# Last pair of experts and three other places reordered in a fused two-block transformer kernel

## The chip, the cores and the metric

The kernel runs on one core of a Trainium2 chip. The core has a matrix engine (PE, whose weight loads are shown as PEld), a vector engine (DVE), a scalar engine (ACT), GpSimd (POOL) and a sync engine (SP) that issues most transfers. The metric is device time in microseconds of one execution of the whole program. All arithmetic is on fp32 data.

## The reference

256 tokens of 1024 features pass through two transformer blocks. The parts that the change touches:

```python
def first_block(x, mem, ...):
    x = x + hybrid_mixer(rmsnorm(x, norm_mix_g), ...)          # mLSTM and spatial gating
    x = x + memory_cross_attention(rmsnorm(x, norm_x_g), rmsnorm(mem, norm_mem_g), w_xq, w_xkv, w_xo)
    x = x + hierarchical_moe(rmsnorm(x, norm_moe_g), w_rg, b_rg, w_re, b_re, w1, w3, w2)
    return rmsnorm(x, norm_f_g)

def memory_cross_attention(xn, mn, w_xq, w_xkv, w_xo):
    q = xn @ w_xq
    k, v = jnp.split(mn @ w_xkv, 2, axis=-1)                   # 4 column blocks of 512: xkv0 to xkv3
    ...

def hierarchical_moe(xn, ...):     # 32 experts of width 512, top 2 of 8 in the best of 4 groups
    ...
    hb = jax.nn.silu(xb @ w1[e]) * (xb @ w3[e])
    return hb @ w2[e]              # gated, and added back to its token's row of x

def second_block(x, c, ctx, ...):
    ada = jax.nn.silu(c) @ w_ada + b_ada       # 12 column blocks of 512: ada0 to ada11
    hc = modulate(rmsnorm(ctx), csh1, csc1); kv_c = hc @ w_in[:, OFF_K:OFF_G]
    ...                                        # Hyena convolution, differential attention, SwiGLU
```

## The kernel before

**Units and the ring.** The weights come in units of 2 MB (8 blocks of 128 rows, 512 columns). `weight_units` lists them in the order in which SP loads them into a ring of five places; unit i of the part before the experts stands in place i mod 5, and its load waits until the unit five before it has been read. SP issues in program order.

**Split products.** Most products are done in three terms, with the weights and the activations each split into a high and a low part in a faster fp32 format. A unit is handled in four quarters: ACT writes the high part (`split_high`, line 2211), DVE the difference (`split_low`, line 1378), PE multiplies (`split_quarter`, line 544). The activations are split likewise, ACT first (2216), then DVE (1384). The high parts of four quarters fit at a time, so ACT makes a quarter's high part when PE has read the quarter four before it.

**Banks.** There are eight PSUM banks. Outside the experts PE takes them in turn, one for each job, in the order in which the jobs are written. It waits, at the head of its queue, until the job eight before has been read out:

```python
def take(name, bank=None):
    b = jobs[0] % 8 if bank is None else bank
    ...
    if n:
        pe.wait_ge(bank_free[b], n)
```

`split_quarter` takes the banks of both its jobs ahead of the first quarter. The jobs around the first place of the change are, in PE's order: memT0 to memT3, adaA0, adaA1, adaB0, mx00, mx01, mx10, mx11, adaA2, adaB1, adaA3, adaB2, xk0_0, xk0_1, adaB3, xk1_0, xk1_1, xv0_0, xv0_1. A job adaA is one column block of the modulation (`ada_part`, 16 matmuls at line 633), adaB its reduction over four row groups (`ada_sum`, 644 or 647), which ACT's copy (`ada`, 2360) comes between and DVE's `ada` (1540) reads. The mx jobs are the spatial gating, read by DVE at line 1587; xk and xv are keys and values of the memory. DVE copies the banks of xk out at line 1630, two after each four low parts of a unit of xkv.

**Queries.** `turn(xT, ...)` transposes the two token tiles of the normalised x (line 598), DVE scales them (1419), both engines split them, and `xq0` multiplies.

**The experts.** 32 experts run as 16 pairs, 64 slots for each expert. For pair n PE does `up(n, 0)` (the two products of the first expert, lines 955 and 956), `scatter(n-1, 0)` (adds the first 512 columns of the pair ahead to the tokens, 1006), `slots_turned` (938) and `turned(n, 0)` (965), `scatter(n-1, 1)`, `up(n, 1)`, the gather of the next pair (929), `turned(n, 1)`, and `down(n)` (975), which computes output columns 0 to 511 (half 0) over all four blocks of the hidden width (k), then columns 512 to 1023. After each half ACT makes the high part of the result (`high`, 2507) and DVE the low (`low`, 1885); the scatter multiplies both by the selection matrix (`picked`), and DVE adds each 128x512 result to x (`acc`, 1901). ACT and DVE stand between up and turned (`h`, 2494) and between turned and down (`sil`, 2500; `hid`, 1877).

A pair has six units of 2 MB in seven places. The loads of the units 7 to 18 are halved, and their first half is let go by the semaphore `half`, which PE raises in the middle of an `up` or `down` of pairs 0 and 1; for `down` that is after k = 1 of half 1. The last pair has no gather behind it, and its `w2` comes in four pieces for each expert (`last_piece`); `down_by_pieces` (992) runs over k outside and over the halves inside. While the last pair runs, ACT and DVE also split the context's activations (`split_activations(ctx_parts, hcT)`) for the first product of the second block (p4x), which follows on PE at line 544.

Of the kernel before, what the change touches and what calls it, by code (L numbers as in the profile page):

```python
# [28 lines left out]
NT = N // P  # L29
# [8 lines left out]
C = 64  # L38
# [33 lines left out]
def weight_units(w):  # L72

    def cols(a, c0, n=512):
        return a[:, c0:c0 + n].rearrange("(k p) n -> p k n", p=P)

    units = []

    def add(name, *parts):
        units.append((name, parts))  # L80

    def whole(name, view):
        add(name, (lambda u, k=view.shape[1], n=view.shape[2]: u[:, 0:k * n].rearrange("p (k n) -> p k n", k=k), view))

    w_in = w["w_in"][0]
    for j in range(8):
        whole(f"in{j}", cols(w_in, 512 * j))
    for j in range(8):
        whole(f"in{8 + j}", cols(w_in, 4096 + 2 * H + 512 * j))
    whole("ws", w["w_s"][0].rearrange("g t s -> t g s"))  # L90
    def ada_units(a, b):
        for j in range(a, b):
            whole(f"ada{j}", cols(w["w_ada_2"][0], 512 * j))

    def tables(name):
        add(name, *[((lambda u, i=i: u[:, 512 * i:512 * i + 512].rearrange("p (k n) -> p k n", k=2)),
                     w["dft"][i].rearrange("(p k) n -> p k n", k=2)) for i in range(2)],
            *[((lambda u, i=i: u[:, 512 * i:512 * i + N]), w["dft"][i][0:P, :]) for i in (2, 3)])
    ada_units(0, 4)
    for j in range(4):  # L100
        whole(f"xkv{j}", cols(w["w_xkv"][0], 512 * j))
    for j in range(2):
        whole(f"out{j}", cols(w["w_out"][0], 512 * j))
    ada_units(4, 7)
    for j in range(2):
        whole(f"xq{j}", cols(w["w_xq"][0], 512 * j))
    ada_units(7, 9)
    whole("xout0", cols(w["w_xo"][0], 0))
    ada_units(9, 12)
    whole("xout1", cols(w["w_xo"][0], 512))  # L110
    before = len(units)
    w2 = w["w_in_2"][0]
    for name, j in (("p4x", 4), ("p5x", 5), ("p0", 0), ("p1", 1)):
        whole(name, cols(w2, 512 * j))
    add("hT")
    for j in (2, 4):
        whole(f"p{j}", cols(w2, 512 * j))
    tables("dftB")
    for j in (3, 5, 6, 7, 8, 9):
        whole(f"p{j}", cols(w2, 512 * j))  # L120
    whole("hyup", w["w_hy_up_2"][0].rearrange("(k p) n -> p k n", p=P))
    whole("attup", w["w_att_up_2"][0].rearrange("(k p) n -> p k n", p=P))
    for j in range(2):
        whole(f"mo{j}", cols(w["w_out_2"][0], 512 * j))
    for j in range(FC // 2):
        add(f"gu{j}", *[((lambda u, i=i: u.rearrange("p (k i n) -> p k i n", k=KD, i=2)[:, :, i, :]),
                         cols(w[nm][0], 256 * j, 256)) for i, nm in enumerate(("w_ffn_gate_2", "w_ffn_up_2"))])
    for j in range(-(-FC // 4)):
        r0, r1 = 512 * j, min(512 * j + 512, DFF)
        whole(f"dn{j}", w["w_ffn_down_2"][0][r0:r1, :].rearrange("(k p) n -> p k n", p=P))  # L130
    return units, before


def two_blocks(nc, w, out):
# [18 lines left out]
    with ExitStack() as ctx:  # L153
# [316 lines left out]
        def _(pe):  # L470
# [276 lines left out]

            ada_part(2)
            ada_sum(1)
            ada_part(3)  # L750
            ada_sum(2)
            split_features("xk0", "xkv0", mem_parts, halves_split(12))
            ada_sum(3)
            split_features("xk1", "xkv1", mem_parts)
            for j in range(2):
                split_tokens(f"xv{j}", f"xkv{2 + j}", mem_parts)
            pe.wait_ge(s["comb_ready"], 1)
# [29 lines left out]
            ada_part(4)  # L787
            turn(xT, hat2, hats=4, tiles_of=(0,))
            ada_part(5)
            ada_part(6)  # L790
            ada_sum(4)
            turn(xT, hat2, hats=4, tiles_of=(1,))
            ada_sum(5)
            ada_sum(6)
            split_features("xq0", "xq0", x_parts, halves_split(20))
# [150 lines left out]
            def halved(n):  # L946
                return isinstance(n, int) and n < HALF_PAIRS
# [20 lines left out]
            def down(n):  # L968
                w2u = [loaded(n, 3 * j + 2).rearrange("p (k n) -> p k n", k=KF) for j in range(2)]
                reach(pe, moe["hid"], 2 * n + 2)  # L970
                for half in range(2):
                    reach(pe, moe[f"low{half}"], n)
                    for k in range(KF):
                        for j in range(2):
                            mm = pe.matmul(PS[4 + half][j * C:(j + 1) * C, :], hidT[:, j, k, :],  # L975
                                           w2u[j][:, k, half * 512:(half + 1) * 512], start=(k == 0), stop=(k == KF - 1),
                                           skip_group_check=True)
                        if half and k == KF // 2 - 1 and halved(n):
                            mm.then_inc(moe["half"], 1)
                    mm.then_inc(moe["down"], 1)  # L980

            def down_by_pieces(n):

                w2u = [moe_place((WHOLE + j) % PLACES).rearrange("p (k n) -> p k n", k=KF) for j in range(2)]
                reach(pe, moe["hid"], 2 * n + 2)
                for half in range(2):
                    reach(pe, moe[f"low{half}"], n)
                for k in range(KF):
                    pe.wait_ge(last_piece[k], 32)
                    for half in range(2):  # L990
                        for j in range(2):
                            mm = pe.matmul(PS[4 + half][j * C:(j + 1) * C, :], hidT[:, j, k, :],
                                           w2u[j][:, k, half * 512:(half + 1) * 512], start=(k == 0), stop=(k == KF - 1),
                                           skip_group_check=True)
                        if k == KF - 1:
                            mm.then_inc(moe["down"], 1)

            def scatter(n, half):

                reach(pe, moe["picked"], n + 1)  # L1000
                reach(pe, moe[f"y{half}"], n + 1)
                reach(pe, moe[f"low{half}"], n + 1)
                for t in range(NT):
                    reach(pe, moe["acc"], 4 * n + max(2 * half + t - 1, 0))
                    for part in range(2):
                        mm = pe.matmul(PS[6 + t][:, :], selT[:, t * P:(t + 1) * P], yB[part][:, half * 512:(half + 1) * 512],  # L1006
                                       start=(part == 0), stop=(part == 1))
                    mm.then_inc(moe["scattered"], 1)

            def step(n, col, after, before):  # L1010
# [5 lines left out]
                    spectrum(7, 7)  # L1016
                slots_turned(n)
                turned(n, 0)
                if after:
                    scatter(n - 1, 1)  # L1020
                up(n, 1)
                if before:
                    gather(n + 1, 0)
                turned(n, 1)
                if before:
                    gather(n + 1, 1)
                    down(n)
                else:
                    down_by_pieces(n)
                if not after:  # L1030
                    banks_free(6, 7)
# [332 lines left out]
        def _(dve):  # L1364
# [217 lines left out]
            for t in range(NT):  # L1582
                for i in range(2):
                    ps = full(dve, f"mx{t}{i}")
                    for j in range(4):
                        g = 4 * i + j
                        did(dve.scalar_tensor_tensor(out=U[:, t, g * P:(g + 1) * P], in0=ps[:, j * P:(j + 1) * P], scalar=bs[:, g:g + 1],
                                                     in1=U[:, t, g * P:(g + 1) * P], op0=ALU.add, op1=ALU.mult),
                            free(f"mx{t}{i}") if j == 3 else None, hold=(j == 3))

            dve.wait_ge(s["G_ready"], 8)
            ada(0)
            ada(1)
            split_low(1)
            split_activations(mem_parts, actT, (1, 3))
            split_low(3)
            ada(2)
            split_low(2)
# [293 lines left out]
                did(dve.tensor_tensor(even, even, odd, ALU.add))  # L1892
                did(dve.scalar_tensor_tensor(out=odd, in0=odd, scalar=-2.0, in1=even, op0=ALU.mult, op1=ALU.add))

            def acc(n):
                for half in range(2):
                    for t in range(NT):
                        reach(dve, moe["scattered"], 4 * n + 2 * half + t + 1)
                        reach(dve, moe["acc"], 4 * n)
                        xs = x[:, t, half * 512:(half + 1) * 512]  # L1900
                        dve.tensor_tensor(xs, xs, PS[6 + t][:], ALU.add).then_inc(moe["acc"], 1)  # L1901

            def step(n, col, after, before):
                if after:
                    acc(n - 1)
                picked(n)
                hid(n, 0)
                if not before:
                    split_activations(ctx_parts, hcT)
                if before:  # L1910
                    select(n + 1, col + 2)
                    xg(n + 1, 0)
                hid(n, 1)
                if before:
                    xg(n + 1, 1)
                low(n, 0)
                low(n, 1)
                if n in (2, 3):
                    spectra_of_halves(n - 2)
                if not before:  # L1920
                    acc(n)

            def alone(n, col):
                select(n, col)
# [263 lines left out]
        def _(act):  # L2188
# [175 lines left out]
            memT = [f"memT{i}" for i in range(4)]  # L2364
            full(act, "memT3")
            split_activations(memT, mem_parts, actT, (0, 2, 1, 3))
            ada(2)
            split_high(2)
            ada(3)
            split_high(2 + 12)  # L2370
            def values(j, tiles_of=range(NT)):
                for t in tiles_of:
                    nm = f"xv{j}_{t}"
# [614 lines left out]
```

## Time and profile before

| what | value |
|---|---|
| median of 3 runs | 1299.24 us (1298.53 to 1300.81) |
| the profiled execution, its own time | 1300.37 us |
| its span, first to last instruction | 1298.6 us |
| PE busy | 1261.2 us (97%) |
| DVE / ACT / POOL busy | 698.1 / 509.3 / 102.9 us |
| moved by transfers | 362.89 MB, mean 279 GB/s |
| mean granted clock of PE | 0.998 |

The profiled execution took 1.13 us more than the median run, and 1.8 us of its time lie outside the span. Busy PE means that some matmul was under way, at whatever rate. The time in a row is counted from the first instruction.

### The profile page before, as it was taken

To read this page: it belongs to the slowest core of one execution; us is meant where nothing else is said; L and a number is where in the kernel's file an instruction comes from. 1 tells how busy PE (TensorE), PEld (TensorE's weight loads), DVE (VectorE), ACT (ScalarE), POOL (GpSimd) and SP (SyncE) were. 2 spreads that over 40 slices of the span, in tenths; PEclk is the share of its full clock that TensorE was granted. 3 is DMA by queue.
4 is the path that set the end of the run, shared out by engine and by line. 5 is a ranking of instruction groups with operands and counts; after the bars stand their busy time and mean duration, and the time that the engine had idled before them with its cause. 6 is when DMAs were issued, how large, how long until landed. Compare 5 with 4: busy or idle time off the path is not lost.

```text
span 1298.6 us, 17828 instructions
## 1 busy us (share of the span) xinstructions
PE 1261.2 (97%) x7053; PEld 887.4 (68%) x7053; DVE 698.1 (54%) x1169; ACT 509.3 (39%) x778; POOL 102.9 (8%) x111
## 2 busy tenths in 40 slices
PE   8999999999999999999999999999999999999998
PEld 7987886976776444444445444449966787899986
DVE  5675668667664323322322222247996868855552
ACT  5556674345244111111111111137344685644442
POOL 6740200200000000000000000000043000000000
PEclk9999999999999999999999999999999999999999
DMA  9654747958876999999999999995416254655440
GB/s 350 240 193 140 251 151 262 371 180 292 308 283 238 402 424 426 426 427 428 429 428 427 425 429 427 427 397 199 154 65 221 104 201 140 194 167 169 184 162 33
DMA packets 103316, 362.89 MB, mean 279 GB/s; under 512 B 4306, under 2 KB 28373, under 8 KB 89600
## 3 DMA queue, kind: packets, MB, share of 16 engines
q1 hardware_dynamic: 99872, 352.60, 70.0%
q0 software_dynamic: 3168, 9.06, 2.2%
q8 instruction: 59, 0.97, 0.3%
q14 instruction: 25, 0.20, 0.0%
q10 hardware_dynamic: 192, 0.06, 0.0%
HBM read 360.65 MB, written 1.05 MB: 279 GB/s over the span
## 4 chain that ended last, share of the span: by engine, by line
PE 85%; DVE 7%; ACT 3%; issue 2%; DMA 1%; POOL 1%; ACTq 0%; DVEq 0%; POOLq 0%
PE bank L544 37%; PE bank L955 17%; PE bank L975 8%; PE bank L929 5%; PE bank L1330 5%; PE bank L1006 3%; DVE ring_parts L1378 2%; PE bank L965 1%; ACT ring_parts L2211 1%; DMA ring<-in_w_xkv 1%; PE bank L633 1%; PE bank L956 1%; PE bank L1170 1%; PE bank L598 1%; PE bank L831 1%
## 5 line engine op out<-in xcount | busy, mean ns | idle before, releaser
L1378 DVE TENSOR_TENSOR ring_parts<-ring,ring_parts 128x1024 fp32r<-128x1024 f32 x202 | 243.6, 1227 | 128.7 <-ACT ring_parts L2211 125.8
L2211 ACT ACTIVATE ring_parts<-ring 128x1024 fp32r<-128x1024 f32 x222 | 230.0, 1057 | 189.6 <-PE bank L544 164.7
L544 PE MATMUL bank<-ring_parts,arena_parts 128*128 128x512 f32 x1056 | 272.3, 393 | 4.1 <-ACT ring_parts L2211 1.5
L544 PEld LDWEIGHTS bank<-ring_parts,arena_parts 128*128 128x128 f32 x1056 | 196.6, 188 | 48.6 <-ACT ring_parts L2211 2.8
L544 PE MATMUL bank<-arena_parts,ring_parts 128*128 128x256 f32 x1504 | 199.4, 285 | 3.0 <-DVE ring_parts L1378 1.8
L955 PE MATMUL bank<-ring,arena 128*64 128x512 f32 x432 | 190.6, 594 | 8.2 <-issue 8.2
L956 PE MATMUL bank<-ring,arena 128*64 128x512 f32 x448 | 197.9, 595 | 0.0
L544 PEld LDWEIGHTS bank<-arena_parts,ring_parts 128*128 128x128 f32 x1504 | 191.4, 193 | 5.1 <-issue 3.3
L955 PEld LDWEIGHTS bank<-ring,arena 128*64 128x64 f32 x432 | 57.5, 137 | 126.7 <-issue 126.7
L2494 ACT ACTIVATE arena<-bank 128x512 f32<-128x512 f32 x32 | 19.1, 597 | 227.4 <-PE bank L956 227.4
L975 PE MATMUL bank<-ring,arena 128*64 128x512 f32 x416 | 106.3, 596 | 0.0
L544 PE MATMUL bank<-ring_parts 128*128 128x512 f32 (+1 forms) x496 | 103.6, 346 | 0.7 <-issue 0.7
L1901 DVE TENSOR_TENSOR x<-x,bank 128x512 f32<-128x512 f32 x64 | 41.1, 684 | 102.3 <-PE bank L1006 102.2
L544 PEld LDWEIGHTS bank<-ring_parts 128*128 128x128 f32 x496 | 79.7, 190 | 15.2 <-issue 5.3
L544 PE MATMUL bank<-ring_parts,flank_parts 128*128 128x512 f32 (+1 forms) x256 | 81.7, 364 | 0.1
L1865 DVE TENSOR_TENSOR arena<-bank,gmoe 128x512 f32<-128x512 f32 x32 | 22.1, 691 | 108.7 <-PE bank L929 108.7
L1885 DVE SCALAR_TENSOR_TENSOR arena_parts<-bank,stat,arena_parts 128x512 fp32r<-128x512 f32 x32 | 24.0, 751 | 101.7 <-ACT arena_parts L2507 101.6
L2507 ACT ACTIVATE arena_parts<-bank,stat 128x512 fp32r<-128x512 f32 x32 | 22.0, 687 | 123.1 <-PE bank L975 116.2
L975 PEld LDWEIGHTS bank<-ring,arena 128*64 128x64 f32 x416 | 32.8, 137 | 53.5 <-issue 52.0
L929 PEld LDWEIGHTS bank<-arena 128*128 128x128 f32 x512 | 59.6, 192 | 13.5 <-issue 13.5
L929 PE MATMUL bank<-arena 128*128 128x128 f32 x512 | 63.9, 279 | 0.5 <-DVE arena L1850 0.5
L1330 PE MATMUL bank<-ring_parts,arena_parts 128*128 128x512 f32 x264 | 60.0, 390 | 0.0
(411 smaller groups left out, 1502.1 us busy)
## 6 DMA issues: line engine op xcount, KB each, us to landing
ring<-in_w SPq DMA_DIRECT2D x70, 2048.0 KB, 20.9
ring<-in_w_in SPq DMA_DIRECT2D x27, 2048.0 KB, 9.7
ring<-in_w_ada SPq DMA_DIRECT2D x12, 2048.0 KB, 8.7
flank<-in_w SPq DMA_DIRECT2D x12, 2048.0 KB, 21.1
ring<-in_w SPq DMA_DIRECT2D x22, 1024.0 KB, 9.9
ring<-in_w_ffn_gate SPq DMA_DIRECT2D x11, 1024.0 KB, 5.3
ring<-in_w_ffn_up SPq DMA_DIRECT2D x11, 1024.0 KB, 8.0
ring<-in_w_ffn_down SPq DMA_DIRECT2D x5, 2048.0 KB, 7.7
```

What stands on the lines that cost most here:

```text
L544: mm = pe.matmul(ps[:, o:o + width], *pair, start=(o == 0 and kk == 0 and ha + hw == 0), stop=(kk == kn - 1 and (ha, hw) == terms[-1] and ...
L929: mm = pe.matmul(PS[half][:, k * P:(k + 1) * P], hat3[:, t, (4 * half + k) * P:(4 * half + k + 1) * P], selB[:, t, :], start=(t == 0), sto ...
L955: pe.matmul(PS[2][0:C, :], xgT[:, k, j, :], w1u[:, k, :], start=(k == 0), stop=(k == KD - 1))
L956: mm = pe.matmul(PS[2][C:2 * C, :], xgT[:, k, j, :], w3u[:, k, :], start=(k == 0), stop=(k == KD - 1))
L975: mm = pe.matmul(PS[4 + half][j * C:(j + 1) * C, :], hidT[:, j, k, :], w2u[j][:, k, half * 512:(half + 1) * 512], start=(k == 0), stop=(k ...
L1006: mm = pe.matmul(PS[6 + t][:, :], selT[:, t * P:(t + 1) * P], yB[part][:, half * 512:(half + 1) * 512], start=(part == 0), stop=(part == 1))
L1330: mm = pe.matmul(accs[t][half][:], act_f[:, t * P:(t + 1) * P], wts[:, 0, half * 512:(half + 1) * 512], start=(f == 0 and n == 0), stop=(f ...
L1378: dve.tensor_tensor(low, src, high, ALU.subtract).then_inc(low_ready, 1)
L1865: dve.tensor_tensor(xgT[:, 4 * half:4 * half + 4].rearrange("p k b c -> p k (b c)"), PS[half][:].rearrange("p (k c) -> p k c", k=KD // 2), ...
L1885: dve.scalar_tensor_tensor(out=yB[1][:, c], in0=PS[4 + half][:], scalar=slot_gate, in1=yB[0][:, c], op0=ALU.mult, op1=ALU.subtract).then_i ...
L1901: dve.tensor_tensor(xs, xs, PS[6 + t][:], ALU.add).then_inc(moe["acc"], 1)
L2211: act.activation(high, src, ACT.Copy).then_inc(high_ready, 1)
```

## The change

Four places of the instruction order are changed; the arithmetic stays the same.

1. Unit xkv0 is loaded ahead of ada3. PE does xk0 ahead of `ada_part(3)`; the sums of ada2 and ada3 stand ahead of the second quarter of xk0 and xk1. DVE makes the low part of the first quarter of xkv0 between the two token tiles of mx, and splits the other two memory activations ahead of `ada(0)` and `ada(1)`. ACT's high parts stand otherwise around its copies of ada2 and ada3.
2. The second token tile of x is transposed ahead of `ada_part(6)` and `ada_sum(4)`.
3. In pairs 0 and 1 the down product runs over k outside (`down_by_rows`), so that the first half of `w2` has been read after half of it, where `half` is raised.
4. In the last pair the two tiles of `scatter(14, 1)` stand behind `up(15, 1)` and behind `turned(15, 1)`; the down product runs over the column halves outside; DVE's order is rewritten (`last_step`).

```diff
-    ada_units(0, 4)
-    for j in range(4):
+    ada_units(0, 3)
+    whole("xkv0", cols(w["w_xkv"][0], 0))
+    ada_units(3, 4)
+    for j in range(1, 4):
         whole(f"xkv{j}", cols(w["w_xkv"][0], 512 * j))
...
             ada_part(2)
             ada_sum(1)
+            memory_arrived = halves_split(12)
+
+            def summed(j, arrived=None):
+                def between(q):
+                    if arrived is not None:
+                        arrived(q)
+                    if q == 1:
+                        ada_sum(j)
+                return between
+            split_features("xk0", "xkv0", mem_parts, summed(2, memory_arrived))
             ada_part(3)
-            ada_sum(2)
-            split_features("xk0", "xkv0", mem_parts, halves_split(12))
-            ada_sum(3)
-            split_features("xk1", "xkv1", mem_parts)
+            split_features("xk1", "xkv1", mem_parts, summed(3))
...
             ada_part(5)
+            turn(xT, hat2, hats=4, tiles_of=(1,))
             ada_part(6)
             ada_sum(4)
-            turn(xT, hat2, hats=4, tiles_of=(1,))
             ada_sum(5)
...
             def down(n):
                 w2u = [loaded(n, 3 * j + 2).rearrange("p (k n) -> p k n", k=KF) for j in range(2)]
                 reach(pe, moe["hid"], 2 * n + 2)
+                if halved(n):
+                    down_by_rows(n, w2u)
+                    return
...
-                        if half and k == KF // 2 - 1 and halved(n):
-                            mm.then_inc(moe["half"], 1)
...
+            def down_by_rows(n, w2u):
+
                 for half in range(2):
                     reach(pe, moe[f"low{half}"], n)
                 for k in range(KF):
-                    pe.wait_ge(last_piece[k], 32)
                     for half in range(2):
                         for j in range(2):
...
                         if k == KF - 1:
                             mm.then_inc(moe["down"], 1)
+                        elif half and k == KF // 2 - 1:
+                            mm.then_inc(moe["half"], 1)
...
+            def down_by_pieces(n):
...
+                for half in range(2):
+                    reach(pe, moe[f"low{half}"], n)
+                    for k in range(KF):
+                        if half == 0:
+                            pe.wait_ge(last_piece[k], 32)
+                        for j in range(2):
...
+                    mm.then_inc(moe["down"], 1)
...
-                if after:
+                if after and before:
                     scatter(n - 1, 1)
                 up(n, 1)
                 if before:
                     gather(n + 1, 0)
+                else:
+                    scatter(n - 1, 1, (0,))
                 turned(n, 1)
                 if before:
                     gather(n + 1, 1)
                     down(n)
                 else:
+                    scatter(n - 1, 1, (1,))
                     down_by_pieces(n)
...
+                if t == 0:
+                    split_low(1)
+
+            split_activations(mem_parts, actT, (1, 3))
             dve.wait_ge(s["G_ready"], 8)
             ada(0)
             ada(1)
-            split_low(1)
-            split_activations(mem_parts, actT, (1, 3))
             split_low(3)
             ada(2)
...
+            def last_step(n):
+                acc(n - 1, (0,))
+                hid(n, 0)
+                acc(n - 1, (1,), (0,))
+                hid(n, 1)
+                acc(n - 1, (1,), (1,))
+                picked(n)
+                split_activations(ctx_parts, hcT)
+                low(n, 0)
+                low(n, 1)
+                acc(n)
...
             split_activations(memT, mem_parts, actT, (0, 2, 1, 3))
+            split_high(2)
             ada(2)
-            split_high(2)
+            split_high(4)
             ada(3)
-            split_high(2 + 12)
+            split_high(10)
```

## Rows read from the trace of the kernel before

**Rows 1.** The page, part 4: the chain that ended last, by engine.

```profile
PE 85%; DVE 7%; ACT 3%; issue 2%; DMA 1%; POOL 1%; ACTq 0%; DVEq 0%; POOLq 0%
```

**Rows 2.** Timeline of PE, 221 to 252 us (start, length, instructions, idle before).

```profile
221.80 1.92 PE L633 MATMUL bank<-ring,scT 128*32 128x512 f32 x16
...
226.11 0.47 PE L544 MATMUL bank<-arena_parts,ring_parts 128*128 128x256 f32 x2 [1.81 <-DVE ring_parts L1378]
...
251.13 0.63 PE L544 MATMUL bank<-ring_parts,arena_parts 128*128 128x512 f32 x2
```

**Rows 3.** A window: length, PE, PEld, DVE, ACT, POOL, granted clock, DMA share, GB/s.

```profile
228.00:232.00 4.00, 4.00 (x25) 4.00 (x25) 3.13 (x6) 1.06 (x1) 0.00 (x0) 0.63 1.05 385
```

**Rows 4.** The load of ada3: its issue, and its time to landing.

```profile
L2860 SPq DMA_DIRECT2D ring<-in_w_ada x1: 368/368/368, 209.1 to 209.1; - x1
...
DMA to landing us min/median/max: 8.1/8.1/8.1
```

**Rows 5.** Timeline of DVE, 216 to 255 us.

```profile
216.48 1.29 DVE L1384 TENSOR_TENSOR flank_parts<-flank,arena_parts 128x512 fp32r<-128x512 f32 x2 [1.72 <-ACT arena_parts L2216]
217.69 4.60 DVE L1587 SCALAR_TENSOR_TENSOR arena<-bank,cols,arena 128x128 f32<-128x128 f32 x16
222.33 0.19 DVE L1540 TENSOR_REDUCE adaT<-bank 128x8 f32<-128x32 f32 x1
...
252.43 1.23 DVE L1378 TENSOR_TENSOR ring_parts<-ring,ring_parts 128x1024 fp32r<-128x1024 f32 x1 [1.66 <-ACT ring_parts L2211]
253.57 1.41 DVE L1630 COPY arena<-bank 128x512 f32<-128x512 f32 x2
```

**Rows 6.** Timeline of ACT at 251 us.

```profile
251.34 1.06 ACT L2211 ACTIVATE ring_parts<-ring 128x1024 fp32r<-128x1024 f32 x1 [1.82 <-PE bank L544]
```

**Rows 7.** Timelines of PE and ACT, 306 to 308 us.

```profile
306.18 1.04 PE L598 MATMUL bank<-ident,arena 128*128 128x128 f32 x8
...
306.38 0.60 ACT L2360 ACTIVATE arena<-bank 128x512 f32<-128x512 f32 x1 [0.38 <-PE bank L644]
307.54 0.63 ACT L2216 ACTIVATE arena_parts<-flank 128x512 fp32r<-128x512 f32 x1 [0.57 <-DVE flank L1419]
```

**Rows 8.** Windows of 2 us, 436 to 442 us.

```profile
436.00:438.00 2.00, 2.00 (x12) 0.71 (x10) 0.49 (x1) 0.69 (x1) 0.00 (x0) 1.00 1.02 426
438.00:440.00 2.00, 2.00 (x12) 0.58 (x10) 0.27 (x1) 0.00 (x0) 0.00 (x0) 1.00 0.57 160
440.00:442.00 2.00, 2.00 (x12) 0.72 (x10) 0.75 (x1) 0.69 (x1) 0.00 (x0) 1.00 0.86 307
```

**Rows 9.** Timeline of SP's queue, 436 to 441.5 us.

```profile
438.50 2.74 SPq L2872 DMA_DIRECT2D ring<-in_w  x4
```

**Rows 10.** Waits of PE: total, times, longest.

```profile
PE bank L955 <- issue: 10.3, 8, 2.1
```

**Rows 11.** The chain that ended last, pairs 0, 14 and 15 (start, length, what).

```profile
433.16 7.02 PE bank L975 x32
...
840.29 2.10 issue
...
861.58 6.25 PE bank L992 x28
...
868.58 0.76 DVE arena_parts L1885
...
870.32 0.70 DVE x L1901
```

**Rows 12.** Loads for pair 15: one unit of up, four pieces of down.

```profile
L2867 SPq DMA_DIRECT2D ring<-in_w x1: 328/328/328, 829.1 to 829.1; - x1
...
DMA to landing us min/median/max: 23.0/23.0/23.0
...
L2913 SPq DMA_DIRECT2D ring<-in_w x4: 432/432/1748, 842.2 to 843.6; - x4
...
DMA to landing us min/median/max: 14.8/16.8/18.8
```

More of the change, by code:

```diff
@@ L977, in down @@
                                            skip_group_check=True)
-                        if half and k == KF // 2 - 1 and halved(n):
-                            mm.then_inc(moe["half"], 1)
                     mm.then_inc(moe["down"], 1)
-            def down_by_pieces(n):
-                w2u = [moe_place((WHOLE + j) % PLACES).rearrange("p (k n) -> p k n", k=KF) for j in range(2)]
-                reach(pe, moe["hid"], 2 * n + 2)
+            def down_by_rows(n, w2u):
                 for half in range(2):
@@ L996, in down_by_pieces, with scatter @@
                             mm.then_inc(moe["down"], 1)
-            def scatter(n, half):
+                        elif half and k == KF // 2 - 1:
+                            mm.then_inc(moe["half"], 1)
+            def down_by_pieces(n):
+                w2u = [moe_place((WHOLE + j) % PLACES).rearrange("p (k n) -> p k n", k=KF) for j in range(2)]
+                reach(pe, moe["hid"], 2 * n + 2)
+                for half in range(2):
[4 more added lines that the diff above has]
+                        for j in range(2):
+                            mm = pe.matmul(PS[4 + half][j * C:(j + 1) * C, :], hidT[:, j, k, :],
+                                           w2u[j][:, k, half * 512:(half + 1) * 512], start=(k == 0), stop=(k == KF - 1),
+                                           skip_group_check=True)
+                    mm.then_inc(moe["down"], 1)
+            def scatter(n, half, tiles_of=range(NT)):
                 reach(pe, moe["picked"], n + 1)
@@ L1002, in scatter @@
                 reach(pe, moe[f"low{half}"], n + 1)
-                for t in range(NT):
+                for t in tiles_of:
                     reach(pe, moe["acc"], 4 * n + max(2 * half + t - 1, 0))
@@ L1893, in spectra_of_halves, with acc @@
                 did(dve.scalar_tensor_tensor(out=odd, in0=odd, scalar=-2.0, in1=even, op0=ALU.mult, op1=ALU.add))
-            def acc(n):
-                for half in range(2):
-                    for t in range(NT):
+            def acc(n, halves=range(2), tiles_of=range(NT)):
+                for half in halves:
+                    for t in tiles_of:
                         reach(dve, moe["scattered"], 4 * n + 2 * half + t + 1)
@@ L1903, in step @@
             def step(n, col, after, before):
+                if not before:
+                    last_step(n)
+                    return
                 if after:
@@ L1907, in step @@
                 hid(n, 0)
[L1908 to L1912, printed above, removed]
+                select(n + 1, col + 2)
+                xg(n + 1, 0)
                 hid(n, 1)
-                if before:
-                    xg(n + 1, 1)
+                xg(n + 1, 1)
                 low(n, 0)
@@ L1919, in step @@
                     spectra_of_halves(n - 2)
-                if not before:
-                    acc(n)
+            def last_step(n):
[9 more added lines that the diff above has]
+                acc(n)
             def alone(n, col):
```

## The prediction

> **What bounds the kernel now.** The first view is the chain that ended last: 85% of it is PE, the transfers hold 1% [rows 1]. So a stall of PE, or an instruction taken off its queue, counts in full nearly everywhere. The exception is the experts, and the waits of PE show it: the products of `up` wait eight times, 10.3 us in all, for something that is no instruction [rows 10], and the loads explain it: the second up unit of pair 15, issued at 829.1, lands 23.0 us later [rows 12]. In the later pairs PE thus runs ahead of the weights. There the end is set by when the stream of loads last stood still, and that is found in the windows: at 438 to 442 us [rows 8]. The other views are timelines at the four places: who is last before PE's next matmul, and what has to come free for it.
>
> **Place 1, xkv0 ahead of ada3.** Before, PE starts `ada_part(3)` at 221.80, is through with it and the sum of ada2 by 224.30, and stands idle 1.81 us until the first quarter of xkv0 is split at 226.11 [rows 2]. The load of ada3 was issued at 209.1 and landed 8.1 us later, at 217.2 [rows 4]; xkv0 takes that place in the queue, so its data are no longer late. What is late next? xk0 moves two jobs forward in the turn of the banks. Counting eight jobs back, its second bank is now that of adaB0, where it had been one of mx. adaB0 is given back by DVE's `ada(0)`, which stood right behind the 16 operations of mx, at 222.33 [rows 5]. Now there stand ahead of it, from 217.69: eight operations of mx (half of 4.60, 2.30), a low part of a weight quarter (1.23), eight more (2.30), two splits of activations (1.29), and `ada(0)` itself (two operations as that of 0.19, with the gap 0.4), all [rows 5]. That ends at 225.2; the engines' overlap of about 0.1 for each takes off what the semaphore to PE adds. PE waits from 221.8 to 225.2, 3.4 us where it was 1.81: **+1.6 us**. The 2.5 us of `ada_part(3)` and the sum are done later, at the same length.
>
> The granted clock fell behind that idle time: 0.63 in 228 to 232 us [rows 3], that is partly at 1.2 GHz instead of 2.4, and 4.00 x 0.37 = 1.5 us were lost. The idle time becomes longer, so I leave this loss as it is. If the clock held, place 1 would be 1.5 us better.
>
> **The same move, one product on.** Before, xv0 starts at 251.13 with no wait [rows 2]; its second bank had been that of adaA3. Counting back in the new order, eight jobs before xv0_1 stands xk0_0. That bank is emptied by DVE's copy, and the copy stands in DVE's program behind four low parts of xkv2. The fourth can't be early: its high part needs the place of the last quarter of xkv1, which PE reads until the end of xk1. Before, the row of these events is: xk1 ends at 251.13, ACT starts the high part at 251.34 and takes 1.06 [rows 6], DVE's low part starts at 252.43, the two copies at 253.57 with 1.41 for both [rows 5]. PE didn't wait for them then. Now it does, until the first copy ends: 253.57 + 0.70 + 0.1 for the semaphore = 254.4, so xv0 starts 3.25 us behind the end of xk1: **+3.25 us**. Nothing covers it; PE's queue stands at the wait. It can't be less unless DVE's order differs from the program; more, if the clock falls after it.
>
> One row speaks against a second fall: PE waited 2.10 us at 840.29 [rows 11], and the clock in that stage stayed up. 3.25 us is longer than this and than the 1.81 us after which it fell. The Trainium skill (TensorE: Matmul & The Clock Gate, section "Why this matters for your kernels") advises against idle gaps of PE between bursts of matmuls, since the clock then goes back to its lower level; the fall in rows 3 agrees, the 2.10 us gap shows that it isn't every gap. By that rule a second fall would be added to the sum, which is the first rival below.
>
> **Place 2, the second tile of x.** PE's total stays. What decides is the chain to xq0: its first bank is that of xT1, which DVE reads only behind the low part of xT2, and ACT's high part of xT2 stands behind ACT's copy of adaA6. That copy waits for the sum of ada4 (ACT at 306.38, released by PE L644), and 0.60 later the high part could follow; it started at 307.54 [rows 7]. The eight transposes (1.04) now stand ahead of that sum. The copy goes to about 307.4, the high part to 308.0: 0.4 later, and xq0 with it. **+0.4 us**; bounds -0.1 (the transposes' own gain, if the copy were not in the way) and 0.5.
>
> **Place 3, down of pairs 0 and 1 by rows.** The same 32 matmul records at the same price. `half` rises after 8 of 16 products instead of after 12, in the 7.02 us that begin at 433.16 [rows 11]: 1.75 us earlier, at 436.7. SP issued the loads behind it at 438.50 [rows 9]. The stream ran at 426 GB/s until then, and at 160 and 307 in the next two windows [rows 8]: (266 + 119) / 426 x 2 = 1.8 us lost. With the issue at 436.7 the next load starts while the old one still runs. Of the 1.8 us I take **-1.7**; bounds 0 and -1.8. It lasts to the end of the experts, since the later pairs wait for loads [rows 10]. The first half of the result reaches ACT and DVE later; the 7 us of the next `up` hide that.
>
> **Place 4, the last pair.** Taking `scatter(14, 1)` (1 us of PE) from ahead of `up(15, 1)` brings little: that product's second unit lands at 829.1 + 23.0 = 852.1 [rows 12], within 0.1 us of when PE got there before. The two tiles go into the gaps around `turned(15, 1)`, where PE waits for ACT and DVE. I take -0.1; if the unit were early, -1.0. At the end it is different. Before, after the down product (861.58 + 6.25 [rows 11]) both low parts, a scatter tile and the addition follow one another: the second low part ends about when the scatter starts, and the first addition is at 870.32. With the halves outside, the first half's high and low parts and, but for its addition, its scatter run beside the second half. Left are the second half's high part and its low part, which takes the place of the one that ended at 868.58 + 0.76 = 869.34 [rows 11]; the addition follows at once, 1.0 us before 870.32. **-1.05 us** in all. The pieces don't spoil it: the last is issued at 843.6 and lands at most 18.8 later, at 862.4 [rows 12], and half 0 wants it after three quarters of 3.5 us, at 864.1. DVE's four splits for the context move behind `picked`, from idle time into the 3.5 us of the second half; they end just before the first low part. If that cover were gone, up to 0.5 us return.
>
> **Sum.** 1.6 + 3.25 + 0.4 - 1.7 - 1.05 = +2.5 us. The profiled execution took 1300.37 and would take 1302.9; against the median, 1.13 us lower, it is 1299.24 + 2.5 = **1301.7 us**. Within 0.2% (2.6 us) is what a measurement of this kernel can't tell from no change; the forecast stands on that edge.
>
> **Rivals.** (a) The clock falls again behind the second wait, at the price that rows 3 give: 2.5 + 1.5 = +4.0, 1303.2. For it the longer gap, against it the 2.10 us that did no harm. (b) The clock doesn't fall at all: 2.5 - 1.5 = +1.0, 1300.2. (c) Faster, the other side: the move does what the rows of before invite, and xk0 isn't held by a bank. Then PE starts it at 221.8, the 1.81 us and the clock's 1.5 are gone and there is no second wait: -3.3 + 0.4 - 1.7 - 1.05 = -5.7, 1293.6. It decides if `ada(0)` is through by 221.8; the count of eight jobs speaks against it. (d) Place 3 doesn't do what it says, the stream standing still later instead: +4.2, 1303.4. Against it: the loads that follow are issued in pairs while others run.
>
> **How the numbers follow.** The forecast has 0.48; with 1 us to either side of +2.5 it lies on both sides of 2.6, 0.27 within and 0.21 above. (a) 0.22, (b) 0.15, (c) 0.07, (d) 0.08. Faster: 0.07. Within 0.2%: 0.27 + 0.15 = 0.42. Slower: 0.21 + 0.22 + 0.08 = 0.51. The range goes from +2.5 - 1.5 - 0.5 - 0.1 - 0.9 = -0.5 (no fall of the clock, places 2 to 4 at their lower bounds) to +2.5 + 1.5 + 0.1 + 0.85 = +4.95 (a second fall, place 2 at its upper bound, half of place 3), with 0.5 us more on each side, since the three runs of before lie up to 0.7 us below their median and 1.6 above: 1298.2 to 1304.7; (c) and the tails are left out. The forecast's own range is 1300.7 to 1302.7.
>
> **What would show it.** PE idle about 3.4 us before xk0, released by DVE's `ada`; about 3.2 us before xv0, released by DVE's copy at the line that was 1630; xq0 0.4 us later after its transposes; no window below 400 GB/s behind the start of pair 0's down; about 1 us less between the down product and p4x. The prediction is wrong if xk0 starts without a wait, if either bank comes free elsewhere, or if the granted clock does something that the gaps of before don't show.

## The result and the profile after

The changed kernel took 1307.21 us (median of 4 runs, 1306.08 to 1308.14), the kernel before 1299.84 beside it: ratio 1.0056, 95% interval 1.004 to 1.0072. It is slower by 7.4 us where 2.5 was forecast, and outside the range. Its profiled execution took 1308.14 us with a span of 1306.4, against 1298.6. Of the executions in the experiments below one, 1418.64 us at a mean granted clock of 0.849, is left out of its kernel's ratio.

The chain that ended last, by engine (page, part 4). "issue", time for which the profile shows no releaser, has risen from 2% to 3% [rows 1]:

```profile
PE 85%; DVE 7%; ACT 3%; issue 3%; POOL 1%; ACTq 0%; DVEq 0%; POOLq 0%
```

The timeline of PE at place 1. The last column is the idle time before:

```profile
221.04 0.66 PE L649 MATMUL bank<-ident,arena 128*128 128x128 f32 x4
225.11 0.77 PE L546 MATMUL bank<-arena_parts,ring_parts 128*128 128x256 f32 x2 [3.41 <-DVE flank_parts L1411]
...
256.68 0.70 PE L546 MATMUL bank<-ring_parts,arena_parts 128*128 128x512 f32 x2 [3.05 <-issue]
```

Both waits are there, with 3.41 us for 1.81 ahead of xk0 and 3.05 for none ahead of xv0 [rows 2]. The load of xkv0 was issued at 208.9, landed 8.2 us later, at 217.1, and is not what is late. The timeline of DVE says who is:

```profile
217.53 2.28 DVE L1614 SCALAR_TENSOR_TENSOR arena<-bank,cols,arena 128x128 f32<-128x128 f32 x8
219.84 1.23 DVE L1405 TENSOR_TENSOR ring_parts<-ring,ring_parts 128x1024 fp32r<-128x1024 f32 x1
220.99 2.28 DVE L1614 SCALAR_TENSOR_TENSOR arena<-bank,cols,arena 128x128 f32<-128x128 f32 x8
223.30 1.29 DVE L1411 TENSOR_TENSOR flank_parts<-flank,arena_parts 128x512 fp32r<-128x512 f32 x2
224.51 0.18 DVE L1567 TENSOR_REDUCE adaT<-bank 128x8 f32<-128x32 f32 x1
...
254.75 1.22 DVE L1405 TENSOR_TENSOR ring_parts<-ring,ring_parts 128x1024 fp32r<-128x1024 f32 x1 [1.65 <-ACT ring_parts L2248]
255.89 1.41 DVE L1658 COPY arena<-bank 128x512 f32<-128x512 f32 x2
```

xk0 starts 0.2 us after `ada(0)` is through (224.51, and its addition at 224.73 for 0.17), xv0 when the first of the two copies that begin at 255.89 is done. In rows 5 `ada(0)` stood at 222.33. The profile names line 1411 as releaser of the first wait; the runs below decide between it and `ada(0)`.

Windows of 4 us, with the granted clock third from the right:

```profile
224.00:228.00 4.00, 2.89 (x13) 2.92 (x14) 3.63 (x8) 0.00 (x0) 0.00 (x0) 0.50 1.05 387
228.00:232.00 4.00, 4.00 (x27) 4.00 (x26) 1.62 (x4) 1.06 (x1) 0.00 (x0) 0.70 1.05 387
256.00:260.00 4.00, 3.33 (x10) 2.72 (x11) 1.26 (x2) 0.00 (x0) 0.50 (x1) 0.72 0.99 222
260.00:264.00 4.00, 4.00 (x16) 3.25 (x16) 1.23 (x1) 1.06 (x1) 0.00 (x0) 0.86 0.92 351
408.00:412.00 4.00, 4.00 (x7) 1.69 (x6) 3.42 (x19) 2.37 (x3) 0.00 (x0) 0.58 1.05 444
```

Where rows 3 have one fall, there are three: behind the first wait (0.50 is the lower level, 1.2 GHz, throughout), behind the second, and at 408 us in the expert routing, where PE had no idle time.

Place 2, timelines of ACT and PE (the counterpart of rows 7). ACT's copy of adaA6 stands at 314.76; it waits 1.53 us for PE's sum at line 646, and the high part of xT2 follows it at once:

```profile
314.76 0.60 ACT L2397 ACTIVATE arena<-bank 128x512 f32<-128x512 f32 x1 [1.53 <-PE bank L646]
315.26 0.62 ACT L2253 ACTIVATE arena_parts<-flank 128x512 fp32r<-128x512 f32 x1
...
317.31 0.48 PE L546 MATMUL bank<-arena_parts,ring_parts 128*128 128x256 f32 x2 [1.24 <-DVE flank_parts L1411]
```

Counted from the start of the output product behind xv1 (out0, at 275.97 before and 283.19 after), the copy comes 1.16 us later than before, the high part 0.50 later and xq0 0.49 later.

Place 3: the windows behind the down product of pair 0, which began at 442.55, and SP's queue. SP issues 3.6 us after that start, where it was 5.3 [rows 9, 11], and the gap of rows 8 is gone:

```profile
444.00:446.00 2.00, 2.00 (x12) 0.61 (x10) 0.00 (x0) 0.00 (x0) 0.00 (x0) 1.00 1.01 426
446.00:448.00 2.00, 2.00 (x12) 0.68 (x10) 0.00 (x0) 0.00 (x0) 0.00 (x0) 1.00 1.02 414
448.00:450.00 2.00, 2.00 (x12) 0.72 (x10) 0.52 (x1) 1.07 (x2) 0.00 (x0) 1.00 0.98 393
...
446.17 4.24 SPq L2910 DMA_DIRECT2D ring<-in_w  x4
```

Place 4: the chain through the last two pairs (start, length, what):

```profile
841.56 7.02 PE bank L987 x32
848.58 1.75 issue
...
859.20 0.97 issue
...
869.53 7.11 PE bank L1017 x32
876.67 0.70 ACT arena_parts L2545
878.06 0.69 DVE x L1929
878.88 1.24 PE bank L1030 x4
```

The second up unit is now the later one of what `up(15, 1)` waits for: issued at 837.4 it lands 22.7 us later, at 860.1, so the scatter that left its place bought next to nothing.

The differences between the two profiled executions, milestone by milestone (start of each in the timelines or the chain):

| stretch | forecast, us | after - before, us |
|---|---|---|
| up to the end of xk1: first wait | +1.6 | +1.6 |
| the same stretch, clock behind the wait | 0 | +1.1 |
| second wait, ahead of xv0 | +3.25 | +3.05 |
| xv0 to the output product behind (out0), clock | 0 | +1.67 |
| from there to xq0: place 2 | +0.4 | +0.49 |
| expert routing, clock | 0 | +1.70 |
| down of pair 0 to down of pair 15: place 3 | -1.7 | -1.44 |
| down of pair 15 to p4x: place 4 | -1.05 | -0.27 |
| sum (the rest is -0.1) | +2.5 | +7.8 |

The theory: place 1 alone carries the loss, by its two waits and by a fall of the clock behind each. Its rivals: place 3 or 4 costs something hidden, or the waits are held by other instructions than those named.

### The profile page after: what moved, and what is told of

Read it like the earlier page. It is cut to its first block, busy times and chain, and to the rows that moved or that the text cites. A ratio compares the mean times of both kernels' runs of the same rounds, so it can differ in the third digit from the quotient of the medians.

```text
span 1306.4 us, 17830 instructions
## 1 busy us (share of the span) xinstructions
PE 1265.8 (97%) x7053; PEld 889.8 (68%) x7053; DVE 698.0 (53%) x1169; ACT 508.9 (39%) x778; POOL 103.2 (8%) x111
## 3 DMA queue, kind: packets, MB, share of 16 engines
HBM read 360.65 MB, written 1.05 MB: 277 GB/s over the span
## 4 chain that ended last, share of the span: by engine, by line
PE 85%; DVE 7%; ACT 3%; issue 3%; POOL 1%; ACTq 0%; DVEq 0%; POOLq 0%
PE bank L546 37%; PE bank L964 16%; PE bank L987 7%; PE bank L938 5%; PE bank L1357 5%; PE bank L1030 3%; DVE ring_parts L1405 2%; PE bank L635 1%; PE bank L974 1%; PE bank L999 1%; ACT ring_parts L2248 1%; PE bank L600 1%; PE bank L965 1%; PE bank L1197 1%; PE bank L893 1%
## 5 line engine op out<-in xcount | busy, mean ns | idle before, releaser
L964 PE MATMUL bank<-ring,arena 128*64 128x512 f32 x432 | 190.6, 594 | 8.2 <-issue 8.1
L965 PE MATMUL bank<-ring,arena 128*64 128x512 f32 x448 | 197.9, 594 | 0.0
L964 PEld LDWEIGHTS bank<-ring,arena 128*64 128x64 f32 x432 | 57.4, 137 | 125.8 <-issue 125.8
L987 PE MATMUL bank<-ring,arena 128*64 128x512 f32 x352 | 92.1, 595 | 0.0
L965 PEld LDWEIGHTS bank<-ring,arena 128*64 128x64 f32 x448 | 59.7, 137 | 0.0
```

What stands on the lines that cost most here:

```text
L964: pe.matmul(PS[2][0:C, :], xgT[:, k, j, :], w1u[:, k, :], start=(k == 0), stop=(k == KD - 1))
L965: mm = pe.matmul(PS[2][C:2 * C, :], xgT[:, k, j, :], w3u[:, k, :], start=(k == 0), stop=(k == KD - 1))
```

## The experiments

Each kernel ran in several rounds beside the kernel before on the same chip; times are medians, ratios come with their 95% interval.

**Place 1 left out** (places 2 to 4 stay):

```diff
-    ada_units(0, 3)
-    whole("xkv0", cols(w["w_xkv"][0], 0))
-    ada_units(3, 4)
-    for j in range(1, 4):
+    ada_units(0, 4)
+    for j in range(4):
...
```

> The change without place 1 (xkv0 is loaded and multiplied where it was before; places 2 to 4 as in the change). Theory A, place 1 holds the loss (two waits of PE for a bank and the half clock behind each, 2.7 + 3.05 + 1.7 us in the trace, and a fall of the clock in the routing that follows from the later start): 1.0 to 1.5 us below before. Theory B, the loss in the routing (1.7 us) belongs to something else in the change: about 0.4 us above before, with the low clock still at the routing's last matmuls.

1299.51 us, ratio 0.9994 (0.9986 to 1.0003), 0.9 us below the kernel before by the medians. The loss is gone. In the chain of this kernel the first product is also shorter than the kernel before's 13.23, with 1.93 us of idle time ahead of it where the kernel before has 1.81:

```profile
226.66 11.75 PE bank L544 x96
```

So the fall of rows 3 isn't in each execution: of the four kernels here that leave place 1 as it was, two profiles show it (the kernel before and place 4 alone, 13.23 and 13.24 us), two don't (this one and place 3 alone, 11.75).

**Place 1 alone** (the hunks of place 1 put into the kernel before):

> Before with place 1 alone. Theory A: 7.4 to 9 us above before, xk0 starting after an idle time of 3.4 us, xv0 after one of 3.05, and the granted clock under 1 behind both. Theory B (the two waits cost only themselves): 4.7 us above before.

1308.01 us, ratio 1.0057 (1.0041 to 1.0073), as much as the whole change. Its chain:

```profile
225.13 5.46 PE bank L546 x24
...
253.79 3.05 issue
256.85 23.65 PE bank L546 x96
```

The same waits and the same slow products. The eight products of 512 columns in the routing stage take 3.51 us here, as before, and 5.21 in the changed kernel: place 1 doesn't bring that third fall by itself. The chains, before, changed and here:

```profile
399.91 3.51 PE bank L884 x8
...
407.61 5.21 PE bank L893 x8
...
407.37 3.51 PE bank L893 x8
```

**The first bank given back early:**

```diff
                 if t == 0:
-                    split_low(1)
+                    dve.wait_ge(s["G_ready"], 8)
+                    ada(0)
+                    split_low(2)
 
             split_activations(mem_parts, actT, (1, 3))
-            dve.wait_ge(s["G_ready"], 8)
-            ada(0)
+            split_low(1)
             ada(1)
-            split_low(3)
+            split_low(1)
```

> The changed kernel with VectorE's reduction of the first sum ahead of the second half of the mixed banks. Theory: that bank alone held TensorE for 3.4 us; xk0 starts at about 221.7 us with no idle time ahead of it, the clock stays at 1.00 in 220 to 232, and everything up to the second wait comes 3.4 plus 2.6 us earlier; the second wait (3.05 us) and the fall behind it stay; about 1301.5 us beside 1307.2 for the changed kernel, ratio 1.000 to 1.002. Rival: the second half of the activations' low parts (the instruction that the profile names as releaser) holds the product; then xk0 starts no earlier than 224 us and the time is 1306 or more.

1300.74 us, ratio 1.0009 (0.9999 to 1.0018), some 6 us less than the changed kernel (6.5 by the medians, 6.1 by the ratios). The chain:

```profile
221.82 3.04 PE bank L546 x24
...
247.92 3.05 issue
250.97 23.37 PE bank L546 x96
```

xk0 follows the sum ahead of it with no idle time, though the instruction at line 1411 now starts as late as 224.98. The edit also brings the low part of the second quarter forward; the second half of mx, at 222.67, now starts behind xk0 too. What held xk0 was `ada(0)`, and the releaser that the profile named was not it. The first 24 products take 3.04 us instead of 5.46: the clock's fall was worth 2.4 us there. The second wait and its fall stay.

**The key banks copied early:**

```diff
                 if i % 2 == 0:
-                    split_low()
+                    split_low(4 if i else 2)
...
+                if i == 1:
+                    split_low(2)
```

> The change, with one thing moved on DVE: the two copies that empty the banks of xk0 stand ahead of the third and fourth low part of xkv2 instead of behind the fourth. Theory A, xv0 waits for xk0's bank: the wait of 3.05 us ahead of xv0 goes, and with it the low clock behind it (1.7 us), 4.7 us below the change. If only the wait goes and the clock falls all the same: 3.05 us below. Rival, xv0 waits for something else (its weights' high or low parts): same time as the change, or at most 1 us below.

1301.29 us, ratio 1.0002 (0.9993 to 1.0011). The chain runs through the start of xv0 without a break, and what follows comes 4.55 us earlier than in the changed kernel (278.64 for 283.19), 3.05 for the wait and 1.5 for the clock:

```profile
245.33 30.43 PE bank L546 x168
```

**The second wait filled with work.** After the first bank of xv0 is taken, PE writes 26 transposes of the identity into it, which the product overwrites. The wait itself stays:

```diff
                     for n, (job, _) in enumerate(jobs):
                         take(job, None if banks is None else banks[n])
+                        if job == "xv0_0":
+                            stay_busy(26, PS[JOB[job][0]])
```

> The change, with 26 transposes of the identity (some 2.8 us of PE) put into the wait ahead of xv0; the wait itself stays. Theory A, the clock falls because PE stands idle there: the granted clock stays up after it, 1.7 us below the change. Rival, the clock falls for another reason (a phase of its own, or the transposes don't count): same time as the change.

1305.34 us, ratio 1.0032 (1.002 to 1.0044). With transposes in the wait the chain goes through DVE's copy of xk0's bank, where it had only "issue". The product behind the wait is not slow: 22.09 us for 23.63. So the clock's part is a cost of its own, 1.5 us:

```profile
256.19 0.69 DVE arena L1660
...
256.92 22.09 PE bank L546 x96
```

**Both waits filled** (`if job in ("xk0_0", "xv0_0")` in the same edit):

> The changed kernel with 26 transposes of the identity in each of place 1's two waits (into the bank that the waiting product has already been given). Both waits stay as long as they are: xk0 starts at about 225.1 us and xk1 is followed by a wait. Theory: the falls of the clock behind the waits are a cost of their own, 2.6 us behind the first and 1.5 behind the second; with TensorE at work the clock stays at 1.00 in 224 to 232 and 250 to 264 us, the first quarter of xk0 takes 2.9 us instead of 5.46, out0 comes at about 279 us instead of 283.19, and the time is about 1302.5 to 1304 us, ratio near 1.002 (2 us and more still lost to the waits themselves). Rival: such transposes don't hold the clock in the first place, which follows 32-column products; then the first quarter still takes 5 us, out0 comes at 281.8 as with the second wait filled alone, and the time stays at 1305 us.

1307.08 us, ratio 1.0054 (1.0041 to 1.0067): nothing won by the time, where the theory had 1302.5 to 1304. By the trace the first half of the expectation holds: the granted clock is 1.00 in the windows from 220 to 236 and 248 to 264 us, the first 24 products of xk0 take 3.14 us, and the output product starts at 279.30, 3.9 us earlier. This gain is lost 600 us later, in p4x behind the experts. The chain:

```profile
225.15 3.14 PE bank L546 x24
...
874.41 2.94 PE bank L546 x12
877.35 2.50 issue
879.85 9.95 PE bank L546 x36
```

PE stands for 2.50 us after 12 products, in the middle of the second quarter, where the program has no wait (a quarter has eight products here). The granted clock falls to 0.57 behind it, and the other 36 take 9.95 us. A record of 16 KB of the queue that loads instructions lies in the window of 0.1 us that begins at 877.4.

**Fewer transposes** (20 instead of 26 in each wait), and **code alone** (52 transposes of a single element in the first wait, none in the second):

```diff
+                        if job == "xk0_0":
+                            b = PS[JOB[job][0]]
+                            for _ in range(52):
+                                pe.transpose(b[:, 0:1], ident[0:1, :], ident[0:1, 0:1])
```

> As the kernel with 26 transposes in each of the two waits, with 20 in each: 12 instructions less. There the clock stayed at full speed and out0 came 3.9 us earlier, but TensorE stood still for 2.50 us at 877.35 in the first product behind the expert loop, while a block of instructions was on its way, and the clock fell behind it: 4.2 us lost. Theory: that wait is for instructions and goes by where the code lies; with 12 instructions less it moves by 12 products, some 2.9 us later, and is shorter than 1 us or gone; then the time is 1302.5 to 1304 us. Rival: the wait is for data that come too late when the loop ends earlier; then it stays at 877 us with 2.5 us and the time is 1307.

> The changed kernel with 52 transposes of one column of one row in the first of place 1's waits, nothing in the second: as many instructions more as in the kernel with 26 in each wait, with next to no work in them. Theory: the same wait of about 2.5 us stands in the first product behind the expert loop, 12 products after its start, though everything ahead of it is as late as in the changed kernel or nearly so; the time is 1307 to 1311 us, and lower only by what the clock falls less behind the first wait. Rival: without an earlier end of the loop that wait doesn't come, and the stretch from the start of that product to the transposes behind it is 11.2 us as in the changed kernel.

With 20 each: 1303.72 us, ratio 1.0031 (1.0019 to 1.0042), and no wait in p4x. With code alone: 1309.66 us, ratio 1.0078 (1.0063 to 1.0094), and the wait is back, 12 products after the start, though the last down product starts later (866.65) than with 26 in each wait (863.82). The clock doesn't fall behind it, and the other 36 products take 8.47 us. The two chains, fewer transposes first:

```profile
876.10 5.64 PE bank L546 x24
```

```profile
877.22 2.95 PE bank L546 x12
880.17 2.74 issue
```

So the wait goes by the number of instructions ahead, not by when the experts end, and late data don't explain it. In the three kernels the instruction record moves 3.0, 3.1 and 3.1 us after p4x starts, and in the kernel before and the changed one, which don't wait, 3.1 and 3.2 us. That PE waits where it gets to the end of the instructions that it has ahead of this record is argued from these times: with 12 transposes less (each a weight load and a product) it would get there 12 products, about 2.7 us, later, and it doesn't wait.

**Place 3 alone** (`down_by_rows` in the kernel before):

> The kernel before with place 3 alone (the halved pairs' down products run columns outside). Theory: the 1-us gap of the weight stream between 436 and 442 us closes, every load behind it lands earlier, and the late pairs start 1.4 to 1.7 us earlier; with the same wait for the last pair's second up load as the stream allows, the end comes 1.2 to 1.7 us earlier, about 1298.9 us beside 1300.4. Rival: the stream waits for other places anyway, the late pairs start where they did, and the time stays within 0.5 us of the kernel before.

1298.78 us, ratio 0.9987 (0.9978 to 0.9996). From down of pair 0 to down of pair 15 its profile has 427.12 us against 428.42, a gain of 1.3. It is also a fourth kernel with place 1 untouched, and it shows the fall in the routing stage, with the code up to there as before:

```profile
398.47 5.21 PE bank L884 x8
```

So that fall belongs to some executions, not to the change: 4 of 14 profiles here have it (5.21 us for 3.51; the changed kernel, place 3 alone, fewer transposes, and both waits taken away with place 2).

**Place 4 alone** (order of the last pair in the kernel before):

> The kernel before with place 4 alone (the last pair rearranged). Theory, from the trace of the changed kernel: from the start of the last down product to the start of the product behind it 10.6 us instead of 10.9, a gain of 0.2 to 0.3 us, which the time can't show: 1300.2 us beside 1300.4. Rival, as predicted: a gain of 1.05 us in that stretch, hidden in the changed kernel by something that place 3 brings; then the stretch takes 9.8 us here and the time is 1299.3.

1300.33 us, ratio 1.0002 (0.9993 to 1.0011). From the start of the last down product, 861.47, to p4x, 872.08, it takes 10.61 us against 10.89: 0.28 less, as in the whole change (0.27), not 1.05.

**Both waits taken away**, by both edits of DVE's order above, once with place 2 undone and once with it:

> The changed kernel with both waits of place 1 taken away (the first sum reduced early, the first two key banks copied ahead of the third and fourth low part) and place 2 undone. Theory: xk0 starts at 221.7 us without idle time, xv0 follows xk1 without a wait, the clock stays at 1.00 from 220 to 264, out0 comes at about 272.6 us (275.97 before, 283.19 changed), place 3 and 4 give 1.7 more: about 1295.5 us, ratio 0.996 to 0.9975. Rival: another bank or part is late in their place, or the clock falls behind a shorter wait; then out0 comes at 275 us or later and the time is 1298.5 or more.

> The changed kernel with both waits of place 1 taken away, place 2 kept as the change has it. Theory: out0 at 272.7 us as without place 2, xq0 0.4 to 0.5 us later after out0 than with place 2 undone (from out0 to xq0 34.1 instead of 33.6 us), the rest the same: about 1295.8 us, ratio 0.9965 to 0.998. Rival: place 2 costs nothing once the work ahead of it is earlier; then the stretch from out0 to xq0 is 33.6 us.

Without place 2: 1295.35 us, ratio 0.9971 (0.9959 to 0.9984), the fastest here, 4 to 5 us below the kernel before and 11 to 12 below the changed one (by the ratios and by the medians). With place 2: 1296.42 us, ratio 0.997 (0.996 to 0.998), about 4 us below the kernel before. By the profiles, out0 to xq0 takes 33.63 us without and 34.12 with it, so place 2 costs 0.49 us. The chain without place 2:

```profile
221.88 3.04 PE bank L546 x24
...
239.35 30.43 PE bank L546 x168
```

xk0 and xv0 start without a wait, and nothing of the clock is lost in this stretch.

## Why the prediction was wrong

What failed is the price of the clock behind the two waits. The sum put it at nothing beyond the 1.5 us of before; the table has +1.1 and +1.67, together 2.8 of the 5.3 us by which the two profiles miss the forecast. Of the rest, 1.7 is the routing stage and 0.8 is place 4.

- **The two waits: right, in place, releaser and size.** 3.41 and 3.05 us were forecast as 3.4 and 3.25, and each went when its bank was given back earlier, by `ada(0)` and by the copy.
- **The clock behind the first wait: the step that failed.** "The idle time becomes longer, so I leave this loss as it is." It became 2.4 us (5.46 for 3.04 in the first 24 products), against 1.5 in rows 3; and the kernel before doesn't have its 1.5 us in each execution, so against its median the step probably misses more than the 1.1 of the table. The range had no term for it either.
- **The clock behind the second wait: left out of the sum and put into a rival at 0.22; it came each time.** 1.3 to 1.7 us, in every profile that has the wait with PE idle in it (the changed kernel, place 1 alone, the first bank early, code alone), and in none with PE at work. The argument against it was one gap of 2.10 us; that a gap of 1.81 had done harm and the new one was longer than both should have weighed more. The rule of the Trainium skill (TensorE: Matmul & The Clock Gate, "Why this matters for your kernels") against idle gaps between bursts gives the side that came true here.
- **Place 4: mis-sized, -0.27 for -1.05.** The step took 861.58 + 6.25 [rows 11] as the end of the down product. It is the point at which the chain leaves that product for ACT, after 28 of its 32 records; the timeline of before has the whole product, and the two low parts behind it:

```profile
861.58 7.09 PE L992 MATMUL bank<-ring,arena 128*64 128x512 f32 x32 [0.93 <-DVE arena L1877]
...
868.58 1.61 DVE L1885 SCALAR_TENSOR_TENSOR arena_parts<-bank,stat,arena_parts 128x512 fp32r<-128x512 f32 x2 [7.05 <-ACT arena_parts L2507]
```

  The product ends at 868.67, and the second low part at 870.19, 0.6 us behind the start of the scatter and not about with it. With 7.09 for 6.25 the step's gain of 1.05 shrinks to 0.2. What follows the second half (its high part, its low part, the addition) takes 1.4 us in the changed kernel and 1.65 before: the first addition stands 8.53 us behind the start of the product, where it was 8.74. The forecast put it at 7.7.
- **Place 3: right, 0.3 us smaller** (-1.44 for -1.7; -1.3 alone); one window has 393 GB/s where none below 400 was expected. **Place 2: right, by the chain that was named** (+0.49 for +0.4).
- **The routing stage: 1.7 us of the profiled difference that no step could hold.** It comes and goes between executions: place 3 alone has it, the kernel before and place 4 alone, with the same code up to there, don't.

Against the median place 1 alone makes +7.6 us and the three other places -0.9 together; that is 0.7 below the 7.4 of the whole change, which the intervals cover.

## What to carry to other kernels

When a job is moved within a turn of banks, list for it and for the jobs behind it who empties the bank that each inherits, and move that instruction along: two edits of DVE's order turned a loss of 7.4 us into a gain of about 4. Price a wait of some 3 us on PE with the clock's loss behind it, here 1.3 to 2.4 us more. Before taking the end of a chain's piece as the end of a product, compare its count with the product's.

## What the runs showed of the hardware

- Transposes of the identity held the granted clock at 1.00 through both waits: 26 of them in 3.00 us, and also 20 in 2.35 us, which left PE idle for 1.07 us ahead of xk0. The single-element ones, as long (52 in 3.29 us), left it at 0.79 and 0.78 in 224 to 232 us.
- From 60 us on, the 14 profiles have 19 idle times of PE from 1.8 to 2.74 us. Six were followed by a fall (1.81, 2.00, 2.30, 2.34 and twice 2.50), thirteen were not (1.92 to 2.74, among them the 2.10 of [rows 11]). All eight of 3.05 to 3.41 us were. So up to 2.74 us the length alone doesn't say it. In the routing stage the clock fell, in 4 profiles of 14, with no idle time, behind 32 products of 36 columns (3.50 us).
- 52 transposes more in PE's program cost waits of 2.50 and 2.74 us at a place 650 us later, behind the branch that, after the 16 pairs, jumps over the loop for further slots; with 40 more there was no wait. The Trainium skill (Runtime: NRT & Kernel Launch, "Instruction fetch mechanics") says that a taken branch to instructions that aren't loaded yet breaks the fetch ahead, and that such loads are otherwise mostly hidden; the 16 KB record and the wait behind the branch agree with it. What sets the moment at which the block is asked for was not tried.
